# Relative bias rows repeated in memory and read back with a shifted step, without the flip products

## What is computed

```python
bias = bias_tab[t5_bucket(rel)].astype(jnp.float32).transpose(2, 0, 1)
s = jnp.einsum('bqhd,bkhd->bhqk', sl(q), k).astype(jnp.float32) * scale + bias
return jax.nn.softmax(jnp.where(causal, s, -jnp.inf), axis=-1)
```

## Time and profile before

| | us |
|---|---|
| median of three runs | 1088.29 (1087.28 to 1090.58) |
| the profiled execution | 1088.07 |
| its span | 1086.3 |
| TensorE busy | 1010.0 |
| VectorE busy | 713.6 |
| ScalarE busy | 513.7 |
| GpSimd busy | 48.0 |

### The profile page before, as it was taken

One profiled execution on the slowest core, in us unless ns is written; L12 is line 12 of the kernel. 1 busy time (PEld: TensorE's weight loads), 2 busy tenths in 40 slices (PEclk: granted clock), 3 DMA queues, 4 the chain that ended last, 5 costly groups with the idle time before them and its releaser, 6 DMA issues.

```text
span 1086.3 us, 14456 instructions
## 1 busy us (share of the span) xinstructions
PE 1010.0 (93%) x5600; PEld 859.0 (79%) x5600; DVE 713.6 (66%) x1270; ACT 513.7 (47%) x897; POOL 48.0 (4%) x70
## 2 busy tenths in 40 slices
PE   6999888999999899987999999969998869999997
PEld 5877668888888798766888888758776758888886
DVE  3656557887785765547788878657677457666643
ACT  3446424555532345533555553345466355555532
POOL 5100000000000110001000000010000000000000
PEclk9999998999999999999999999989999999999999
DMA  8644028897795463303987869355331027666551
GB/s 280 225 146 124 1 61 247 238 266 220 251 344 170 124 212 118 117 1 91 296 256 217 265 230 344 99 176 179 115 117 40 2 78 194 190 182 182 187 190 39
DMA packets 191699, 184.97 MB, mean 170 GB/s; under 512 B 7130, under 2 KB 161013, under 8 KB 191632
## 3 DMA queue, kind: packets, MB, share of 16 engines
q1 hardware_dynamic: 188576, 175.85, 52.1%
q0 software_dynamic: 2768, 7.87, 2.4%
q10 hardware_dynamic: 288, 0.33, 0.1%
HBM read 182.97 MB, written 1.06 MB: 169 GB/s over the span
## 4 chain that ended last, share of the span: by engine, by line
PE 79%; DVE 12%; ACT 5%; issue 2%; POOL 1%; DMA 1%; SPq 0%; DVEq 0%; POOLq 0%; ACTq 0%
PE ps L1047 23%; PE ps L999 15%; PE ps L1049 10%; PE ps L1379 5%; PE ps L977 4%; PE ps L979 4%; PE ps L978 4%; DVE wl L1754 3%; PE ps L1094 2%; PE ps L1046 1%; PE ps L1116 1%; ACT probs L1524 1%; ACT wh L1500 1%; DVE probs L1969 1%; DMA raw<-in_w_in 1%
## 5 line engine op out<-in xcount | busy, mean ns | idle before, releaser
L1047 PE MATMUL ps<-xhl,wh 128*128 128x512 f32 (+1 forms) x1104 | 378.0, 399 | 6.2 <-DVE xhl L1766 2.8
L1754 DVE TENSOR_TENSOR wl<-raw,wh 128x2048 fp32r<-128x2048 f32 (+5 forms) x147 | 319.6, 2176 | 95.0 <-ACT wh L1500 94.5
L1500 ACT ACTIVATE wh<-raw 128x2048 fp32r<-128x2048 f32 (+5 forms) x147 | 267.8, 1822 | 189.2 <-PE ps L999 108.3
L1049 PE MATMUL ps<-xhl,wl 128*128 128x256 f32 (+1 forms) x966 | 269.0, 278 | 0.0
L1047 PEld LDWEIGHTS ps<-xhl,wh 128*128 128x128 f32 x1104 | 204.3, 193 | 42.6 <-issue 3.4
L1049 PEld LDWEIGHTS ps<-xhl,wl 128*128 128x128 f32 x966 | 187.7, 194 | 5.2
L977 PE MATMUL ps<-wh,xhl 128*128 128x384 f32 (+5 forms) x268 | 97.7, 365 | 13.4 <-DVE wl L1754 8.1
L1835 DVE TENSOR_TENSOR scratch<-ps,scratch 128x256 f32<-128x256 f32 x132 | 55.6, 421 | 58.4 <-ACT scratch L1681 58.4
L1687 ACT ACTIVATE scratch<-scratch 128x256 f32<-128x256 f32 x66 | 27.6, 418 | 138.3 <-DVE scratch L1835 138.2
L978 PE MATMUL ps<-wl,xhl 128*128 128x384 f32 (+5 forms) x268 | 92.0, 343 | 0.0
L979 PE MATMUL ps<-wh,xhl 128*128 128x384 f32 (+5 forms) x268 | 91.9, 343 | 0.0
(11 more groups left out here) (263 smaller groups left out, 1280.4 us busy)
## 6 DMA issues: line engine op xcount, KB each, us to landing
raw<-in_w_down SPq DMA_DIRECT2D x33, 1024.0 KB, 5.0
adaw<-in_w_ada SPq DMA_DIRECT2D x24, 1024.0 KB, 7.5
raw<-in_w_gate SPq DMA_DIRECT2D x44, 512.0 KB, 4.0
raw<-in_w_up SPq DMA_DIRECT2D x44, 512.0 KB, 5.4
raw<-in_w_gate_up SPq DMA_DIRECT2D x44, 512.0 KB, 5.2
raw<-in_w_in SPq DMA_DIRECT2D x12, 768.0 KB, 4.7
raw<-in_w_in SPq DMA_DIRECT2D x8, 1024.0 KB, 5.2
raw<-in_w_o SPq DMA_DIRECT2D x8, 1024.0 KB, 4.9
```

Source lines behind the costliest of these rows:

```text
L1047: ins = mm(o, a[:, v, k, :], xhl[:, :, k, c], start=k == 0, stop=k == KC - 1)
L1049: mm(o[:, 0, :], b[:, v, k, :], xh[:, k, c], start=False, stop=False)
L1500: me.go(activation(wh[:, m % NW, 0:n], raw[:, ITEM[item] % NRAW, 0:n], ACT.Copy), wh_ready)
L1754: me.go(V.tensor_tensor(wl[:, m % NW, 0:n], raw[:, ITEM[item] % NRAW, 0:n], wh[:, m % NW, 0:n].bitcast(F32), ALU.subtract), wl_ready)
```

## The change

The rows are no longer written once but 128 times: `bias_rows` gets a dimension of 128 copies of each row, written by one DMA whose source repeats (`broadcast_to`). The read steps 383 elements per partition, against copies of 384, and begins at element 127. So partition p reads from copy p, one element further to the left than its neighbour, and gets the values that begin at 127 - p: the right order at once. The five `flip` stages, their products, copies, and the constant `flip` (128 of 651 columns) are gone. VectorE waits for the read (`s_bias_in`) ahead of the first `masked`, where TensorE waited in `flip_bias`. `brow` moves from the space of `cbuf` to that of `probs`, so `latent_keys` no longer waits for the write: on ScalarE it waits for the event `brow`, on VectorE for nothing.

```diff
--- before.py
+++ after.py
@@ -69,7 +69,7 @@
 
 def _const_layout():
     at = 0
-    for name, n in (("ident", P), ("flip", P), ("causal", S), ("cos1", TT * 16), ("sin1", TT * 16), ("cos2", TT * 8),
+    for name, n in (("ident", P), ("causal", S), ("cos1", TT * 16), ("sin1", TT * 16), ("cos2", TT * 8),
                     ("sin2", TT * 8), ("cmpmask", TT * 16), ("cmpvalid", TT), ("cmpblock", 8), ("biasscale", 1)):
         CC[name] = (at, at + n)
         at += n
@@ -88,7 +88,6 @@
 
     p = np.arange(P)[:, None]
     put("ident", np.eye(P))
-    put("flip", np.eye(P)[::-1])
     put("causal", np.where(np.arange(S)[None] <= P + p, 0.0, NEG))
     tok = (np.arange(TT)[None, :] * P + p).astype(np.float32)
     inv1 = (np.float32(10000.0) ** (-np.arange(16, dtype=np.float32) / np.float32(16))).astype(np.float32)
@@ -226,8 +225,6 @@
     add(("wl", "win", 3, 0))
     win(3, 1, 1)
     add(("wh", "win", 3, 1), *(("ct", n) for n in range(6)))
-    if L == 0:
-        add(*(("flip", n) for n in range(5)))
     job(0)
     win(4, 0, 0)
     job(1)
@@ -484,8 +481,6 @@
                 put(("ab", L, a[0]), 2 * (a[0] - 3), alt(a[0]))
             elif stage == "ct":
                 aside(("ct", L, a[0]), alt(a[0]))
-            elif stage == "flip":
-                aside(("flip", a[0]), alt(a[0]))
             elif stage == "S":
                 put(("s", L, a[0]), 4, "dve")
             elif stage == "S2":
@@ -625,7 +620,7 @@
             return ctx.enter_context(nc.semaphore(name))
 
         ps = ctx.enter_context(nc.psum_tensor("ps", [P, 8, 512], F32))
-        bias_dram = nc.dram_tensor("bias_rows", [A_H + B_H, 384], F32, kind="Internal").ap()
+        bias_dram = nc.dram_tensor("bias_rows", [A_H + B_H, P, 384], F32, kind="Internal").ap()
 
         raw = sb("raw", [P, NRAW, SLOTW])
         wh = sb("wh", [P, NW, SLOTW], F32R)
@@ -659,6 +654,7 @@
         cbuf_at = place[0]
         cbuf = at("cbuf", [P, TT, 1536])
         cT = at("cT", [P, 3, S])
+        brow = at("brow", [A_H + B_H, 384], F32, place[0])
         probs = at("probs", [P, 4, 384])
         pT = at("pT", [P, 2, 384])
         dmask = at("dmask", [P, 384])
@@ -673,7 +669,6 @@
         rowsA = at("rowsA", [P, P], F32, cbuf_at)
         rowsB = at("rowsB", [P, P], F32, cbuf_at + 512)
         hot = at("hot", [34, 384], F32, cbuf_at + 1024)
-        brow = at("brow", [A_H + B_H, 384], F32, cbuf_at + 1024 + 1536)
         lamin = at("lamin", [P, DEPTH, P], F32, cbuf_at + 4096)
         cst = sb("cst", [P, NCONST])
         fv = sb("fv", [P, N_A + N_B])
@@ -1211,13 +1206,6 @@
                         o = c * S + t * P
                         ins = nc.tensor.transpose(ps[0:CQ, b, o:o + P], cbuf[:, t, col:col + CQ], ident)
                 fill(ins, ("ct", L, n))
-
-            def flip_bias(n):
-
-                pe.wait_ge(s_bias_in, 16)
-                pe.wait_ge(s_cst, 32)
-                b = claim(("flip", n))
-                fill(mm(ps[:, b, :], cv("flip"), bias[:, 2 * n:2 * n + 2, :].rearrange("p h n -> p (h n)"), start=True, stop=True), ("flip", n))
 
             def gain_rows():
 
@@ -1433,8 +1421,6 @@
                         turn_heads(L, *a)
                     elif stage == "ct":
                         turn_latent_heads(L, *a)
-                    elif stage == "flip":
-                        flip_bias(*a)
                     elif stage == "S":
                         scores(L, *a)
                     elif stage == "T":
@@ -1556,7 +1542,7 @@
             def latent_keys(L):
 
                 if L == 0:
-                    act.wait_ge(s_bias_out, 16)
+                    act.wait_ge(ev("brow"), 1)
                 for h in range(2):
                     key = ("ukv", L, 0, h)
                     wait_full(act, key)
@@ -1647,9 +1633,6 @@
                     elif stage == "ct" and alt(a[0]) == "act":
                         key = ("ct", L, a[0])
                         copy(ut[0:CQ, 10 + 2 * a[0]:12 + 2 * a[0], :], ps[0:CQ, U.bank[key], :].rearrange("p (c n) -> p c n", c=2), key)
-                    elif stage == "flip" and alt(a[0]) == "act":
-                        key = ("flip", a[0])
-                        copy(bias[:, 2 * a[0]:2 * a[0] + 2, :].rearrange("p h n -> p (h n)"), ps[:, U.bank[key], :], key)
                     elif stage == "S":
                         exponents(L, *a)
                     elif stage == "T":
@@ -1963,6 +1946,8 @@
             def masked(L, k):
 
                 j, key = JOBS[L][k], ("s", L, k)
+                if L == k == 0:
+                    dve.wait_ge(s_bias_in, 16)
                 wait_full(dve, key)
                 for t in range(TT):
                     a, e = score_cols(j, t)
@@ -2063,8 +2048,6 @@
 
             def latent_keys(L):
 
-                if L == 0:
-                    dve.wait_ge(s_bias_out, 16)
                 for h in range(2):
                     key = ("ukv", L, 1, h)
                     wait_full(dve, key)
@@ -2319,13 +2302,6 @@
                     elif stage == "ct" and alt(a[0]) == "dve":
                         key = ("ct", L, a[0])
                         copy(ut[0:CQ, 10 + 2 * a[0]:12 + 2 * a[0], :], ps[0:CQ, U.bank[key], :].rearrange("p (c n) -> p c n", c=2), key)
-                    elif stage == "flip":
-                        key = ("flip", a[0])
-                        if alt(a[0]) == "dve":
-                            copy(bias[:, 2 * a[0]:2 * a[0] + 2, :].rearrange("p h n -> p (h n)"), ps[:, U.bank[key], :], key)
-                            me.settle()
-                        else:
-                            wait_done(dve, key)
                     elif stage == "S":
                         masked(L, *a)
                     elif stage == "T":
@@ -2403,9 +2379,9 @@
             load_lora(0)
 
             gp.wait_ge(ev("brow"), 1)
-            gp.dma_start(bias_dram, brow[:, :]).then_inc(s_bias_out, 16)
+            gp.dma_start(bias_dram, brow[:, :].unsqueeze(1).broadcast_to([A_H + B_H, P, 384])).then_inc(s_bias_out, 16)
             gp.wait_ge(s_bias_out, 16)
-            gp.dma_start(bias[:, :, :], bass.AP(bias_dram.tensor, bias_dram.offset, [[1, P], [384, A_H + B_H], [1, S]])).then_inc(s_bias_in, 16)
+            gp.dma_start(bias[:, :, :], bass.AP(bias_dram.tensor, bias_dram.offset + P - 1, [[383, P], [P * 384, A_H + B_H], [1, S]])).then_inc(s_bias_in, 16)
             for L in range(DEPTH):
                 power(rs[:, :, 0:2], va[:, :, 0:2], ev("var_lat", L), 1, ev("rstd_lat", L))
                 wait_full(gp, ("ukv", L, 1, 1))
```

## The result

The changed kernel takes 1116.97 us (median of four runs, 1116.52 to 1117.44) against 1089.34 us (four runs, 1087.28 to 1090.58) before: a ratio of 1.0256, interval 1.0236 to 1.0275. It is slower, by 27.6 us in the medians. The profiled executions are 1117.44 and 1088.07 us, their spans 1115.6 and 1086.3.

A forecast was written before the change was run, and what follows sets the result against it. The prediction took TensorE (busy 93% of the span, 79% of the chain) to bound the kernel; flips -4.1, constants -0.2, TensorE's wait for the larger write +28.8 and clock +2.5 gave +27.0, so 1115 us, range 1091 to 1127.

## What to carry to other kernels

Before a DMA is made larger, look at what stands behind its wait in the issuing queue, not only at who needs its data: here the data had 26 us of cover, and an unrelated four-column power behind it had 0.16. Cost a DMA by how its source lies over the partitions, not by its bytes alone: 2 MB took 7.2 us from 128 partitions and 34.3 from ten neighbours, 0.8 MB from four neighbours 34.3 too, and the three weight loads issued while the write from ten partitions ran took 29.6 to 31.6 us each. The reversed order, which cost five products before and 2 MB of copies after, was had here, at no cost that the rows show, by reversing a constant and reading it backwards.

## What the runs showed of the hardware

Four neighbouring partitions together are read by DMA no faster than one alone: 24.5 GB/s for partitions 0 to 3, and 29 for one (196.6 KB in 9.0 - 2.2 us). With the same share of the DMA engines busy, about a quarter, four partitions gave 25, 47 or 89 GB/s by their place. A 768 KB load over all partitions, issued while such a write ran, took 30.6 us in place of 8.0; beside a write of about the same size from 128 partitions it took 6.8. Reading 2.03 MB from 120 partitions took 12.4 us where 1.97 MB from 128 took 7.2; no run here says why. VectorE's masked score reads an operand with a step of -1 in the same 0.29 us as with a step of 1.
